# A decoder step on one core: loads of the first layer reordered, index pages and index products re-slotted, attention's tie-breaking cut into thinner pieces

## What is computed

```python
for l in range(2):
    mk, mv = _mem_kv(mem_prompt, w_mem_kv[l], mem_kn[l])
    if l % 2 == 0:
        xp, (c, n, m), _ = _even_layer(xp, mk, mv, zero_C, zero_n, zero_m, *prm)     # and for the samples
    else:
        xp, (k, v, ki) = _odd_layer(xp, pos_p, mk, mv, _dsa_prompt, *prm)            # samples: _dsa_sample, paged caches

def _index_select(qi, wi, ki, qpos, topk):
    s = jnp.einsum('bqhd,bld->bqhl', qi, ki) * IDX_DIM ** -0.5
    s = jnp.einsum('bqhl,bqh->bql', jax.nn.relu(s), wi)
    s = jnp.where((kpos[None, :] <= qpos[:, None])[None], s, -jnp.inf)
    _, idx = lax.top_k(s, topk)          # ties: the earlier key wins
```

## Time and profile before

| | us |
|---|---|
| median of 3 runs | 1933.82 |
| lowest, highest | 1931.24, 1935.46 |
| the profiled execution's own time | 1932.26 |
| its span in the profile | 1930.7 |
| PE busy, idle in the span | 1802.3, 128.4 |
| mean granted TensorE clock (share of full) | 0.974 |

### The profile page before, as it was taken

How to read it: one execution, slowest core, us unless ns; L and a number is a source line. 1 busy time by engine, 2 the same in 40 slices (tenths; PEclk the granted TensorE clock), 3 DMA queues, 4 the chain that set the end, 5 groups by cost and what they waited for, 6 DMA issues and landing times. The chain is left out here.

```text
span 1930.7 us, 26765 instructions
## 1 busy us (share of the span) xinstructions
PE 1802.3 (93%) x9553; PEld 1396.5 (72%) x9553; DVE 977.6 (51%) x2276; ACT 602.7 (31%) x1274; POOL 412.5 (21%) x646
## 2 busy tenths in 40 slices
PE   6999999999999998998999899999998678999999
PEld 5666788777777876886875556887676466777887
DVE  5512643234376665221532467888786575675211
ACT  3111332111022112200211245877744245554000
POOL 4301221000133352000341101211003355430000
PEclk9999999999899999999999999999999689999999
DMA  6433333443344367321322112333432665322221
GB/s 209 133 108 126 100 111 106 160 165 108 100 145 162 121 196 272 136 94 53 96 63 55 62 39 78 99 107 125 147 126 67 224 213 186 117 91 98 107 106 52
DMA packets 130118, 234.87 MB, mean 122 GB/s; under 512 B 28354, under 2 KB 56546, under 8 KB 129986
## 3 DMA queue, kind: packets, MB, share of 16 engines
q1 hardware_dynamic: 109154, 170.50, 26.8%
q0 software_dynamic: 17328, 56.24, 8.9%
q10 hardware_dynamic: 3504, 6.42, 0.9%
HBM read 166.95 MB, written 66.16 MB: 121 GB/s over the span
## 5 line engine op out<-in xcount | busy, mean ns | idle before, releaser
L1187 PE MATMUL layer_acc<-layer_w_hi,layer_xT_hi 128*128 128x512 f32 x640 | 262.8, 411 | 0.2 <-PE all_banks L1335 0.2
L1189 PE MATMUL layer_acc<-layer_w_hi,layer_xT_lo 128*128 128x512 f32 x640 | 253.8, 397 | 0.0
L1188 PE MATMUL layer_acc<-layer_w_lo,layer_xT_hi 128*128 128x512 f32 x640 | 253.5, 396 | 0.0
L2746 PE MATMUL front_acc<-front_w_hi,front_xT_hi 128*128 128x512 f32 x520 | 219.0, 421 | 16.1 <-DVE front_w_lo L3264 4.9
L2747 PE MATMUL front_acc<-front_w_lo,front_xT_hi 128*128 128x512 f32 x520 | 207.0, 398 | 0.0
L2748 PE MATMUL front_acc<-front_w_hi,front_xT_lo 128*128 128x512 f32 x520 | 206.7, 398 | 0.0
L1187 PEld LDWEIGHTS layer_acc<-layer_w_hi,layer_xT_hi 128*128 128x128 f32 x640 | 122.4, 191 | 30.7 <-issue 5.9
L1188 PEld LDWEIGHTS layer_acc<-layer_w_lo,layer_xT_hi 128*128 128x128 f32 x640 | 121.7, 190 | 26.8 <-issue 2.6
L1189 PEld LDWEIGHTS layer_acc<-layer_w_hi,layer_xT_lo 128*128 128x128 f32 x640 | 121.4, 190 | 27.1
L2746 PEld LDWEIGHTS front_acc<-front_w_hi,front_xT_hi 128*128 128x128 f32 x520 | 99.5, 191 | 48.6 <-issue 8.7
L3062 ACT ACTIVATE front_index_rows<-odd_bias,front_candidate 128x1024 bf16<-128x1024 f32 (+3 forms) x128 | 124.8, 981 | 13.3 <-DVE front_candidate L3356 8.3
(11 more groups left out here) (671 smaller groups left out, 3651.4 us busy)
## 6 DMA issues: line engine op xcount, KB each, us to landing
all_w<-in_w_even POOLq DMA_DIRECT2D x80, 256.0 KB, 3.6
h_even<-layer_st SPq DMA_DIRECT2D x79, 256.0 KB, 2.1
all_w<-in_w_odd POOLq DMA_DIRECT2D x61, 256.0 KB, 3.5
h_odd<-front_st SPq DMA_DIRECT2D x56, 256.0 KB, 2.1
layer_scratch<-h_even SPq DMA_DIRECT2D x46, 256.0 KB, 3.0
all_scratch<-in_w_mem SPq DMA_DIRECT2D x32, 256.0 KB, 3.8
all_scratch<-h_even SPq DMA_DIRECT2D x32, 256.0 KB, 3.6
all_scratch<-x SPq DMA_DIRECT2D x14, 512.0 KB, 3.7
```

The lines of the kernel that those rows point to most:

```text
L1187: T.matmul(out[0:rows, :], xh[:, kk, to], wh[:, r, :], start=(kk == 0), stop=False)
L1188: T.matmul(out[0:rows, :], xh[:, kk, to], wl[:, r, :], start=False, stop=False)
L1189: ins = T.matmul(out[0:rows, :], xl[:, kk, to], wh[:, r, :], start=False, stop=(kk == KC - 1))
L2746: T.matmul(out[0:rows, :], xh[:, k, to], wh[:, r, :], start=(k == 0), stop=False, skip_group_check=True)
```

## The change

It moves steps between slots and between queues; no arithmetic is added or removed.

- First layer: the first two `load_q` go from slot 19 to slot 18, in front of the store of slot 19's unit. In the chunk loop the query rows are loaded one slot sooner (`load_q_rows`), and keys and values come in front of the store of h and the load of the gates.
- Second layer, front: from the fourth sequence on, ACT issues the second four index pages of a sequence, behind its copy; SP issues the first four. The second pair of heads of each of the first six parts is multiplied inside the half unit that follows, after two of its four weight slices.
- Second layer, back: POOL writes the constant before it loads pages. ACT takes the squares of the first prepared tile one slot ahead of its 16 small copies, DVE and POOL handle that tile's sums one slot later. The ties go from 4 slots to 10 in smaller pieces, ACT scales a block in a slot after the last piece. The samples' softmax gets one more slot.

```diff
@@ loads_keys, loads_mem (SP)
+                    if p == 15:
+                        sp.wait_ge(wmf, 16)
+                        sp.wait_ge(xe, 2 * T1)
+                        load_q(0)
+                        load_q(1)
                     yield
             def loads_mem():
-                sp.wait_ge(wmf, 16)
-                sp.wait_ge(xe, 2 * T1)
-                load_q(0)
-                load_q(1)
                 load_g(0)
@@ load_qkv (SP)
+            def load_q_rows(i):
+                t = tile_at(i)
+                if i >= 2:
+                    sp.wait_ge(ltr, i)
+                    sp.wait_ge(*stored_by(unit_of(E_Q, t)))
+                sp.dma_start(q[0:rows_in(t), :], c.h_even[cols_in(t), E_Q:E_Q + CW]).then_inc(l_in[i % 2], 16)
...
-                sp.dma_start(q[0:rows, :], c.h_even[r, E_Q:E_Q + CW]).then_inc(l_in[u], 16)
+                if i < 2:
+                    load_q_rows(i)
@@ loads_chunk (SP)
-                    yield
+                    if i + 2 < T1:
+                        load_q_rows(i + 2)
+                    yield
+                    if i + 2 < T1:
+                        load_qkv(i + 2)
                     if i:
                         store_h(i - 1)
                     if i + 1 < T1:
                         load_gates(i + 1)
-                    if i + 2 < T1:
-                        load_qkv(i + 2)
@@ layer1_front: pages (SP), double (POOL), half and indexes (PE), smps (ACT)
+                for p in range(PAGES if b < PAGED else PAGES // 2):
+                    sp.dma_start(ip[b % PAGED][:, p, :], index_page(sp, b, p)).then_inc(ip_in[b % PAGED], 16)
...
+                pool.wait_ge(ip_in[b % PAGED], (PAGES + b // PAGED * (PAGES // 2)) * 16)
+                if b >= PAGED:
+                    pool.wait_ge(ia_in[b % PAGED], b // PAGED * (PAGES // 2) * 16)
...
+                    if k == KC // 2 * side + 1 and (n, side) in second_pairs:
+                        next(pairs)
...
-                    yield
+                        yield
...
+            second_pairs = [(n, side) for n in range(17, 21) for side in range(2)][1:1 + sum(len(hs) > 2 for _, hs in PARTS)]
...
+                    if b + PAGED < NB:
+                        act.wait_ge(twice, b + 1)
+                        for p in range(PAGES // 2, PAGES):
+                            act.dma_start(ip[b % PAGED][:, p, :], index_page(act, b + PAGED, p)).then_inc(ia_in[b % PAGED], 16)
@@ back_plan
-    for s in range(1, 39):
+    for s in range(1, 40):
         plan[s].append("smp")
-    for s in (3, 5, 7, 9):
+    for s in (3, 5, 7, 9, 10, 11, 13, 15, 17, 18):
         plan[s].append("ties")
@@ layer1_back: preps (POOL)
+                G.memset(minus[:, :], -SC).then_inc(made, 1)
                 load_last_k(2)
                 load_last_k(3)
-                G.memset(minus[:, :], -SC).then_inc(made, 1)
...
-                        at = step - (p > 2)
+                        at = step - 1
@@ layer1_back: preps (ACT), in its second slot; the small copies follow in the third
+                yield
+                first_squares(2)
                 yield
                 act.wait_ge(made, 2)
@@ layer1_back: preps (DVE)
-                        if step == (0 if p == 2 else 1):
+                        if step == 1:
@@ layer1_back: late_biases (ACT), late_ties (DVE)
-                    yield
+                    for _ in range(4):
+                        yield
                     act.wait_ge(chosen, n + 1)
...
                     link(V.tensor_scalar(e, v, at, 0.0, ALU.is_equal, ALU.add, accum_out=ties[:, :]))
+                    yield
                     link(V.tensor_tensor_scan(m, e, e, 0.0, ALU.add, ALU.max))
                     yield
...
                     link(V.scalar_tensor_tensor(m, m, need[:, 0:1], e, ALU.is_gt, ALU.mult))
+                    yield
                     link(V.scalar_tensor_tensor(v, v, at, m, ALU.is_lt, ALU.max))
                     dve.sem_inc(chosen, 1)
+                    yield
                     yield
```

More of the change, by code:

```diff
@@ L2338, in layer1_front @@
             s.sem("evacuated_by_dve"), s.sem("tanhs"), s.sem("stored", ST))
-        parts, whole = s.sem("sample_parts"), s.sem("sample_whole")
+        parts, whole, ia_in = s.sem("sample_parts"), s.sem("sample_whole"), s.sem("idx_pages_by_act_in", PAGED)
         x_in, small_in, wk_d, wkd, rope_in = (s.sem("x_in", 2), s.sem("small_in"),
@@ L2394, in own_rows, with index_page @@
             return slice(SMP * g, SMP * g + SMP)
+        def index_page(eng, b, p):
+            page = eng.value_load(c.page_ids[0:1, PAGES * b + p:PAGES * b + p + 1], min_val=0, max_val=a["cache_idx_k"].shape[1] - 1)
+            return a["cache_idx_k"][0, bass.ds(page, 1)].rearrange("o s d -> (o s) d")
         @block.sync
@@ L2428, in pages @@
                     sp.wait_ge(twice, b - PAGED + 1)
-                n_pool = a["cache_idx_k"].shape[1]
-                for p in range(PAGES):
-                    at = PAGES * b + p
-                    page = sp.value_load(c.page_ids[0:1, at:at + 1], min_val=0, max_val=n_pool - 1)
-                    src = a["cache_idx_k"][0, bass.ds(page, 1)].rearrange("o s d -> (o s) d")
-                    sp.dma_start(ip[b % PAGED][:, p, :], src).then_inc(ip_in[b % PAGED], 16)
+                for p in range(PAGES if b < PAGED else PAGES // 2):
+                    sp.dma_start(ip[b % PAGED][:, p, :], index_page(sp, b, p)).then_inc(ip_in[b % PAGED], 16)
             def loads_smp():
@@ L2622, in double @@
             def double(b):
-                pool.wait_ge(ip_in[b % PAGED], (b // PAGED + 1) * PAGES * 16)
+                pool.wait_ge(ip_in[b % PAGED], (PAGES + b // PAGED * (PAGES // 2)) * 16)
+                if b >= PAGED:
+                    pool.wait_ge(ia_in[b % PAGED], b // PAGED * (PAGES // 2) * 16)
                 if b >= 2:
@@ L2948, in first_heads @@
                     yield
-            follow_halves(plan, UNITS, half, amid, norm=norms(), prep=preps(), smp=smps(), index=indexes(), find=idle(), mem=mems(), cached=cacheds(),
+            second_pairs = [(n, side) for n in range(17, 21) for side in range(2)][1:1 + sum(len(hs) > 2 for _, hs in PARTS)]
+            pairs = indexes()
+            follow_halves(plan, UNITS, half, amid, norm=norms(), prep=preps(), smp=smps(), index=pairs, find=idle(), mem=mems(), cached=cacheds(),
                           qk=first_heads(), copy=idle(), cached_copy=idle(), decide=idle())
@@ L3794, in load_v @@
                         sp.dma_start(vp[b][:, p, :], value_page(sp, b, p)).then_inc(vq_in[b // 2 - 1 if b < 7 else 0], 16)
-                for u in range(UNITS + 6):
+                for u in range(UNITS + 7):
                     if u + KRING < UNITS:
@@ L4186, in _, with first_squares @@
             A = nc.scalar.activation
+            def first_squares(p):
+                u, rows = p % 2, rows_in(PREP[p])
+                act.wait_ge(qk_in[u], 16 * (p // 2))
+                if p > 2:
+                    act.wait_ge(red, p - 2)
+                A(sq[0:rows, :], qk[u][0:rows, :], ACT.Square).then_inc(squ, 1)
             def preps():
@@ L4200, in preps @@
                 A(kT[:, :, cols_in(L)], heads(c.banks[:, 1536 + QH * SMP:1536 + H10 * SMP], KVH), ACT.Copy).then_inc(qcp, 1)
-                for todo in STEPS[1:]:
+                for todo in STEPS[2:]:
                     for p, step in todo:
@@ L4205, in preps @@
                         if step == 0:
-                            act.wait_ge(qk_in[u], 16 * (p // 2))
-                            if p > 2:
-                                act.wait_ge(red, p - 2)
-                            A(sq[0:rows, :], qk[u][0:rows, :], ACT.Square).then_inc(squ, 1)
+                            first_squares(p)
                         j = step - TURN[p]
```

## The result

| | us |
|---|---|
| changed kernel, median of 4 runs | 1908.73 (1907.71 to 1910.72) |
| kernel before, median of 4 runs | 1932.80 |
| ratio, with its 95% interval | 0.9872 (0.9858 to 0.9886) |
| forecast, range | 1897, 1887 to 1912 |
| span in the profile, before and after | 1930.7, 1906.6 |

The account below looks back on a forecast made before the run. PE, busy 1802.3 of 1930.7 us, was taken as the bound, leaving idle time and slow clock to win. Terms summed to 36.7 us off the profiled 1932.3, giving 1895.6; the median 1.5 higher, 1897; range 1887 to 1912.

Parts of the forecast that it names:

- memory queries and slow stretch behind them: First layer: earlier query loads remove PE's whole 4.5 us wait and 2.1 us of slow clock behind it.
- chunk loop: First layer: earlier q, k, v loads remove all but one 0.5 us wait; later gates cost nothing; 5.7 us, bounds 0 to 6.2.
- index pages: Second layer's front: sharing page issue between SP and ACT saves 6.5 us of waits and 1.7 of slow clock.
- index products: Second layer's front: four waits covered, 4.8 us; three merge into one of about 3; possible clock fall counted at -0.8.
- attention: Second layer's opening: earlier maximum, ties in pieces, extra softmax slot and 1.9 us of clock; 12.2 us, bounds 2 to 18.
- Rival (c): Chunk loop: k and v also wait for the running slot's update and land no sooner; 1903 us, chance 0.06.
- rival (e): Index pages: ACT's page issue, above 1.22 us a page, delays PE; 1943 us at 3.5 a page, chance 0.03.
- rival (d): Index pages bring nothing, since transfers and POOL's doubling set the pace, not SP's issue; 1905 us, chance 0.05.
- the forecast's own sign of being right: Attention: PE's waits at L4010, the transposes of sample keys, would be under 8 us in sum, from 16.2.
- the forecast's own sign of being wrong: Anywhere in the kernel: PE's waits growing in lines that the change doesn't touch; no size given.
- Rival (a): Attention's opening: the ring's next member takes up what the pieces free, only the first 3 us stay; 1906 us, chance 0.21.
- outside these places PE runs on as before: Whole kernel: each edit is priced by the wait it ends, with PE unchanged elsewhere; no gain or loss counted there.

Follow-up runs that it names:

- x1: The kernel before with only the first-layer edits (memory query loads and chunk-loop loads moved): 1921.11 us, ratio to before 0.9934.
- x9: The changed kernel with attention's ties in four lumps as before: 1912.93 us, ratio to the kernel before 0.9878.
- x10: The changed kernel with the preparation of tiles 2 to 7 begun one slot sooner on every engine: 1915.64 us, ratio to the kernel before 0.9905.
- x12: The changed kernel run again without any edit: 1912.17 us, ratio to the kernel before 0.9878.
- x4: The kernel before with the first-layer and index edits, attention's opening as before: 1912.73 us, ratio to before 0.9893.
- x6: The changed kernel with POOL's multiplication by the gains left out for tiles 2 to 7 (result incomplete): 1908.09 us, one execution.
- x8: The changed kernel without the additional slot in the samples' softmax: 1909.73 us, ratio to the kernel before 0.9864.
- x11: The changed kernel with the preparation of tiles 2 to 7 begun two slots sooner: 1910.20 us, ratio to the kernel before 0.9876.
- x7: The kernel before with POOL's multiplication by the gains left out for tiles 2 to 7 (result incomplete): 1937.67 us, one execution.

## Why the prediction was right, and where it was not

The forecast's way and range held; of the 36.7 us, 24.1 came. Term by term, in the profiled execution:

| step | forecast | measured |
|---|---|---|
| memory queries and slow stretch behind them | 6.6 | 6.8 |
| chunk loop | 5.7 | 7.4 |
| rest of the first layer | 0 | -2.2 |
| output projection, up to the pages | 0 | +1.2 |
| index pages | 8.2 | 8.0 |
| index products | 4.0 | 4.5 |
| later in the second layer's front | 0 | -2.8 |
| attention | 12.2 | 1.2 |
| sum | 36.7 | 24.1 |

**Memory queries** were right in every part: no wait at L1283 (then L1272), full clock.

**Chunk loop**: the mechanism was right, the size above its own upper bound of 6.2. All six waits went, that of 0.5 too, and each of the three longest was worth some 0.2 us more than its listed length (1.88 for 1.67, 1.97 for 1.76, 1.80 for 1.58): the first matmuls behind a wait cost more than the wait. The gates, one microsecond later, cost nothing there. Rival (c) fell. The 7.4 is not what every execution has: of the ten profiles with this edit six gave 7.3 to 7.4 us, and four (x1, x9, x10, x12) 5.6 to 5.8, with 3.4 us at the lower clock where the wait at 557.55 had been. Elsewhere the first layer gave back 2.2, of which 1.6 in the gated MLP behind the loop, where PE waited 2.25 for its load and 1.19 for POOL, against 1.26 and 0.56:

```profile
724.37 1.53 PE L1527 MATMUL all_banks<-all_ident,layer_scratch 128*128 128x128 f32 x12 [2.25 <-DMA layer_scratch<-y_even]
...
727.09 1.16 PE L1517 MATMUL all_banks<-all_scratch,layer_scratch 128*128 128x128 f32 x8 [1.19 <-POOL all_scratch L1168]
```

In x1 that place lost 0.2, in x4 0.6 and in x12 0.2, so the 1.6 are not fixed to the edit.

**Index pages**: right, mechanism and size. ACT paid no more than the nearest row had: 1.05 us from the start of one page to the next (3.52 us for the four), against SP's 1.10, and under the 1.22 from which rival (e) starts.

```profile
1011.57 3.52 ACTq L3059 DMA_DIRECT2D odd_bias<-in_cache_idx_k  x4
...
1011.40 4.74 SPq L2445 DMA_DIRECT2D odd_bias<-in_cache_idx_k  x5
```

By the rule of the Trainium skill that was weighed ("DMA: Bandwidth & Descriptors", section "Issuing engines are not separate DMA queues": only the sequencer's time is saved, usually small) the part would have been worth about nothing. The same bytes went through two issuing engines and 8.0 us were saved, 8.0 too with the index edits alone (x2): rival (d) fell, and the exception that the rule leaves with "usually" is this loop, where 16 pages of issue outlast PE's work on two sequences.

**Index products**: right in the mechanism, and lucky in the clock. One wait of 2.7 us stood where "about 3" was forecast, the others are gone, and 4.5 were won. The prediction could not tell whether this wait would put the clock down and counted half of 1.7 us for it. It did in half of the profiles. In all ten with the index edits the wait is there and 2.74 to 2.75 us long; five had no time at the lower clock behind it and won 4.5, two (x6, x12) had 3.4 us and won 3.0, three (x4, x8, x11) had 6.8 us and won 1.6 to 1.7. The same stretch, from behind the pages to the end of the products, in the changed kernel and in x4:

```profile
1052.86:1103.81 50.95, 48.20 (x207) 26.62 (x205) 31.74 (x56) 19.76 (x35) 3.27 (x8) 1.00 0.11 39
1052.85:1106.66 53.81, 51.06 (x206) 27.80 (x204) 31.77 (x56) 19.77 (x35) 3.30 (x8) 0.94 0.11 37
```

**Attention** is the step that failed: 12.2 us forecast, 1.2 measured. The first maximum came 2.5 us sooner (forecast 2.7), the fourth exponential 2.4 (2.8), that of job 11 9.0, where the forecast's items up to there, without the clock, make 10.5; everything behind job 11 came to -7.9. The step that was wrong is that each item was priced by the wait in which it ended, at full length, and the items were added. From the place late in the front to the end of the span PE was idle 52.5 us before and 50.7 after: 1.8 us less, where the items without the clock have 10.3; and it was busy 0.7 us longer. The waits that were priced did shrink, L4010's from 16.2 to 10.0 (the forecast's own sign of being right was under 8) and the softmax wait of 3.2 to nothing, but waits that stood at nothing in the sum took their place: the value matmuls behind "issue" grew by 5.1 us, 3.1 of it at the matmul shown above, and the rotated tile waits 3.5 for POOL. Waits that grow in lines that the change doesn't touch were the forecast's own sign of being wrong. The prediction weighed DVE's and ACT's queues behind each item, and POOL's not at all past its memset. Its columns in the view above show 23.09 us busy of 51.0 and 25.10 of 45.5 before the change, and page issues cost it 1.15 us each from start to start where 0.54 counts as busy.

The clock was the second thing. The prediction took 7 us at the lower level, behind PE's two longest waits, and 1.9 us of gain from it. The view has 30.6 us at the lower level in jobs 0 to 11, and they did not go but moved: to 16.1 there and 13.7 in jobs 11 to 24. That is why the lead came so close to the forecast by job 11 (of its 9.0 us 5.1 are PE's busy time and 3.9 idle) and was lost again (5.6 of the 7.0 us are busy time). Rival (a), 1906, was the nearest: it said that the next member takes up what the pieces free. It let 3 us stay where 1.2 did. The whole stayed inside the range because its upper end had been set beyond rival (a).

**Later in the second layer's front** nothing was changed and 2.8 us went. PE's wait there was as before; the clock fell behind it, which it had not. Changed kernel, then before:

```profile
1315.93 1.09 PE L2933 MATMUL all_banks<-all_ident,front_index_rows 128*128 128x128 f32 x8 [2.32 <-DMA front_index_rows<-in_cache_mem_k]
...
1318.36 0.63 PE L2760 MATMUL front_acc<-front_w_lo,front_xT_hi 128*128 128x512 f32 x1
```

```profile
1341.75 1.09 PE L2918 MATMUL all_banks<-all_ident,front_index_rows 128*128 128x128 f32 x8 [2.19 <-DMA front_index_rows<-in_cache_mem_k]
...
1344.53 0.40 PE L2748 MATMUL front_acc<-front_w_hi,front_xT_lo 128*128 128x512 f32 x1
```

The stretch (1316.8 to 1406.7) had 6.8 us at the lower clock. It was there again in x12 (3.4) and in all ten profiles of kernels with the index edits (3.4 to 10.2); of the four without them three had none, and x7 had 10.2. So it goes with the index edits mostly, not always, and why stays open. The prediction's phrase "outside these places PE runs on as before" has to be given up for the clock.

## What to carry to other kernels

Price each stall where it stands, but before adding the prices up over a ring of engines, put every engine's whole queue beside the new pace, issues of transfers included: a wait that is taken away comes back where the next queue is full. A wait that vanishes from the list is no proof of a gain; compare the start of the same instruction in both traces, place by place, and see whether the lead stays. Then split the lead of each stretch into the busy and the idle time of the engine that bounds it. If the same instructions take another busy time, the clock has moved, and the wait list has nothing to say about that part. For the idle part, test by taking work away from the suspect in both kernels: if it helps only in the new one, it is a new limit; moving its deadline or its order only moves the wait.

## What the runs showed of the hardware

**The clock is the scatter.** In the first layer between 326 and 548 us, where the code is as before in every kernel, the granted clock was 0.92 to 0.95 over the 14 profiles, some 20 to 34 us at the lower level, and the stretch took 218.6 to 228.0 us. In x12 it was 34 and 226.5 us, in the first profile of the same kernel 24 and 221.7. The medians of the same kernel on two chips, 1908.73 and 1912.17, differ by 3.4 us. So one profile's span says little about 5 us of an edit, and the starts just ahead of the edit and just behind it say more than both medians.

**What the lower level costs.** At the index products, where the same matmuls run behind the same wait, 6.8 us at the lower level cost 2.9 us (53.81 against 50.95) and 3.4 us cost 1.5 or 1.6.

**A wait's length did not decide on the clock.** The wait of 2.75 us at L2848 was followed by a stretch at the lower level in five profiles and by full clock in the five others, the changed kernel among these; x12 is the same kernel as the latter and had 3.4 us. The wait of L2933 was followed by a fall at 2.32 us in the changed kernel and by none at 2.82 us in x12, nor at 2.19 in the kernel before. The Trainium skill's "TensorE: Matmul & The Clock Gate", Part 1, which lets an idle PE fall to half rate, agrees in kind; which gaps are followed by a fall is told by no row here.
